# Down weights of the experts in 8 KB runs, with the expert block turned two columns apart

## What is computed

```
aff = softmax(h @ w_router);  gate, idx = top_k(aff.T, cap)      # cap = 2 * N / 16: 64 latent, 32 context
xe  = h[idx]                                                     # tokens of one expert
hid = silu(xe @ w_gate) * (xe @ w_up)                            # w_gate, w_up: 1024 x 1024
ye  = hid @ w_down * gate                                        # w_down: 1024 x 1024
y[idx] += ye
```

## Time and profile before

| what | value |
|---|---|
| median of 3 runs | 3875.69 us |
| lowest, highest | 3872.78, 3879.06 us |
| the profiled execution's own time | 3871.78 us |
| its span | 3869.7 us |
| DMA traffic of the weight stream's queue | 492.93 MB, 36.3% of 16 engines' span |
| expert loop of layer 0, layer 1 | about 1380 to 2310 us, 3283 to 3813 us |

### The profile page before, as it was taken

How to read it: one execution, slowest core, us unless ns; L and a number is a source line. 1 busy time by engine, 2 the same in 40 slices (tenths; PEclk the granted TensorE clock), 3 DMA queues, 4 the chain that set the end, 5 groups by cost and what they waited for, 6 DMA issues and landing times. The chain is left out here.

```text
span 3869.7 us, 40283 instructions
## 1 busy us (share of the span) xinstructions
PE 3226.1 (83%) x16642; PEld 2182.8 (56%) x16642; DVE 1115.7 (29%) x2003; ACT 550.4 (14%) x1054; POOL 449.7 (12%) x366
## 2 busy tenths in 40 slices
PE   7979996787879899999999984899946666899994
PEld 2545573787866386777776742665735563333331
DVE  0024422545424401111111114172047623111113
ACT  0133115222211100000000001041031200100010
POOL 0000000544403000000000003000026420000002
PEclk9979997899988689999999986999978785999998
DMA  9210112000014265566665650211100010999993
GB/s 303 92 39 17 34 45 86 1 1 1 1 49 131 76 217 192 200 223 212 214 229 190 214 192 24 63 33 33 55 22 1 11 44 15 383 382 362 388 378 142
DMA packets 200206, 512.50 MB, mean 132 GB/s; under 512 B 13200, under 2 KB 97424, under 8 KB 199696
## 3 DMA queue, kind: packets, MB, share of 16 engines
q1 hardware_dynamic: 192880, 492.93, 36.3%
q10 hardware_dynamic: 6048, 13.57, 1.0%
q0 software_dynamic: 1152, 4.19, 0.3%
HBM read 506.99 MB, written 3.67 MB: 132 GB/s over the span
## 5 line engine op out<-in xcount | busy, mean ns | idle before, releaser
L1961 PEld LDWEIGHTS bank<-arena,ring 128*128 128x128 f32 x4096 | 472.5, 195 | 34.5 <-issue 33.5
L1961 PE MATMUL bank<-arena,ring 128*128 128x96 f32 x4096 | 475.3, 278 | 0.8 <-DVE arena L2032 0.8
L1105 PE MATMUL bank<-arena 128*128 128x128 f32 x2208 | 271.9, 284 | 21.4 <-DVE arena L1277 19.7
L1105 PEld LDWEIGHTS bank<-arena 128*128 128x128 f32 x2208 | 264.3, 199 | 27.9 <-issue 24.6
L450 PE MATMUL bank<-arena,ring 128*128 128x384 f32 (+1 forms) x704 | 243.6, 509 | 8.9 <-DVEq L2287 7.5
L2100 PE MATMUL bank<-ring,arena 128*64 128x512 f32 x1024 | 233.4, 599 | 15.3 <-DMA ring<-in_moe_w_up_dram 8.3
L2040 DVE TENSOR_TENSOR arena<-arena,bank 128x512 f32<-128x512 f32 x160 | 110.0, 688 | 451.8 <-PE bank L1945 451.8
L1945 PE MATMUL bank<-arena 128*128 128x512 f32 (+1 forms) x320 | 187.3, 668 | 62.8 <-DVE arena L2040 60.1
L1991 PE MATMUL bank<-ring,arena 128*96 128x512 f32 x512 | 232.6, 606 | 2.2 <-DVE arena L2055 2.2
L1925 PE MATMUL bank<-arena,X 128*128 (+1 forms) x1024 | 165.9, 312 | 55.3 <-DVE arena L2032 26.6
L1925 PEld LDWEIGHTS bank<-arena,X 128*128 128x128 f32 x1024 | 143.7, 215 | 104.6 <-issue 35.0
(11 more groups left out here) (294 smaller groups left out, 3789.9 us busy)
## 6 DMA issues: line engine op xcount, KB each, us to landing
ring<-in_moe_w_gate_dram SPq DMA_DIRECT2D x128, 1024.0 KB, 5.1
ring<-in_moe_w_up_dram SPq DMA_DIRECT2D x128, 1024.0 KB, 5.3
ring<-in_moe_w_down_dram SPq DMA_DIRECT2D x128, 1024.0 KB, 7.0
ring<-in_w_mod_dram SPq DMA_DIRECT2D x48, 1024.0 KB, 5.3
ring<-in_odd_w_in_dram SPq DMA_DIRECT2D x16, 1024.0 KB, 5.6
ring<-in_even_w_in_dram SPq DMA_DIRECT2D x10, 1024.0 KB, 5.3
ring<-in_even_w_out_dram SPq DMA_DIRECT2D x4, 1024.0 KB, 5.4
arena<-in_rpb_tables_dram POOLq DMA_DIRECT2D x8, 512.0 KB, 4.5
```

The costliest lines, as they stand in the source:

```text
L1105: mm = nc.tensor.matmul(heads(out[:, :])[:, h, :], lhs(h), rhs(h), start=start, stop=stop)
L1961: mm = nc.tensor.matmul(bank[x + f // 4][:, (f % 4) * M:(f % 4 + 1) * M], wslot(c)[:, kk, f * P:(f + 1) * P], xe[:, k, :], start=k == 0 an ...
```

## The change

Down chunks are read so that partition p holds rows 2p and 2p + 1 of the chunk's 256, which lie next to each other in HBM: 8 KB in one run instead of two runs of 4 KB. For the down product the hidden features have to stand in the same order. `hidden_rows(f)` gives them: of each 256 hidden columns, the even ones for the first block and the odd ones for the second. In layer 0 the stationary blocks of gate and up (line 1961) are taken with it, in layer 1 the transposes' inputs (line 2116). Gate and up chunks are read as before. The products, their number and order, the waits and the slots are the same.

```diff
                 flat = t[w].rearrange("l e (k p) n -> (l e) p k n", p=P)
-                src = flat[bass.ds(l * NE + 2 * i + e, 1), :, 2 * c:2 * c + 2, :].rearrange("a p k n -> (a p) k n")
+                if w == "moe_w_down":
+                    rows = t[w].rearrange("l e (k p r) n -> (l e) p k r n", p=P, r=2)
+                    src = rows[bass.ds(l * NE + 2 * i + e, 1), :, c, :, :].rearrange("a p r n -> (a p) r n")
+                else:
+                    src = flat[bass.ds(l * NE + 2 * i + e, 1), :, 2 * c:2 * c + 2, :].rearrange("a p k n -> (a p) k n")
...
+            def hidden_rows(f):
+
+                return slice(f // 2 * 2 * P + f % 2, (f // 2 + 1) * 2 * P, 2)
...
                                     mm = nc.tensor.matmul(bank[x + f // 4][:, (f % 4) * M:(f % 4 + 1) * M],
-                                                          wslot(c)[:, kk, f * P:(f + 1) * P], xe[:, k, :],
+                                                          wslot(c)[:, kk, hidden_rows(f)], xe[:, k, :],
                                                           start=k == 0 and f % 4 == 0, stop=k == KB - 1 and f % 4 == 3)
...
-                            mm = nc.tensor.transpose(bank[5][:, b_ * P:(b_ + 1) * P], HID2[:, b_ * P:(b_ + 1) * P], ident)
+                            mm = nc.tensor.transpose(bank[5][:, b_ * P:(b_ + 1) * P], HID2[:, hidden_rows(b_)], ident)
```

## The result

The changed kernel takes 3903.14 us (median of 4, 3901.66 to 3909.53) against 3874.24 us for the kernel before (4 runs, 3871.91 to 3879.06): ratio 1.0076, 95% interval 1.0059 to 1.0094, so 23 to 36 us slower, where 3875.0 us and "no change" were forecast, with a range up to 3886. The execution shown here is the one of 3901.66 us, with a span of 3899.7 us.

A forecast was written before the change was run, and what follows sets the result against it. TensorE was taken to bound layer 0, and layer 1 nearly everywhere in a near tie with transfers. Median 3875.69 us + 0 (weight-load stride) + 0 (transposes) - 0.7 (down chunks) = 3875.0 us, range 3864 to 3886.

The forecast's parts named there:

- Part 1: Layer 0's up/gate weight loads, 4096 on TensorE's path: reading columns two apart was taken to cost 0.
- the ends of 0 and 457 us: Bounds for layer 0's 4096 strided loads: free, or twice the reading time at +0.1115 us each, +457 us.
- The partial end: Layer 0's strided weight loads costing 2% of a load-and-matmul pair, 4096 x 0.0022 = +9 us.
- Part 2: Layer 1's transposes, 64 strided loads of 141 ns: taken as free, +9 us if doubled.
- Part 3: Down chunks in runs of 8 KB, 64 a layer: 0.09 us saved a chunk, 0.7 us in all, layer 1 only.
- The pause in the steady pair: Layer 1, DMA engines nearly idle about 5 us a pair of experts; shorter down chunks would lengthen it about 0.4 us.
- The 0.7 us: Layer 1's saving: 8 down chunks ahead of waits, in the first pair and at the very end, 0.09 us each.
- the strided weight load is slower: Rival: layer 0's 4096 strided loads cost time on the path, up to 4341 us at full price; chance 0.14.
- The transfers gain far more: Rival: 8 KB packets or better HBM order remove layer 1's 15.2 us of weight waits, 3860.5 us; chance 0.07.
- arrive slower: Rival: down chunks take +0.20 us each, +13 us if all 64 are on the path, 3889 us; chance 0.03.
- nothing merges: Rival: down chunk runs stay 4 KB, so transfers don't change, 3875.7 us; chance 0.10.

The follow-up runs named there:

- e2: Changed kernel with down chunks back in runs of 4 KB, so both strides alone: 3896.97 us, ratio 1.0079 to the kernel before.
- e1: Changed kernel with both strides taken out, so down chunks in runs of 8 KB alone: 3866.26 us, ratio 0.9999 to the kernel before.
- e3: Kernel before with the stationary blocks of line 1961 taken with a step of four columns: 4491.00 us, ratio 1.1613.
- e11: Kernel before with the moving operand of line 1991 (512 columns) taken with a step of four columns: 4111.49 us, ratio 1.0628.

## Why the prediction was wrong

**Part 1, the stride in the weight loads, is the step that failed.** The place was right: 4096 loads on the path, multiplied without cover. Its price wasn't 0 but 6.2 ns a pair, 25 us, between the ends of 0 and 457 us; the interval of the whole loss, 23 to 36 us, holds it. I took the value from VectorE (2% within 9 ns, rows 6) as "the same memory read with the same 8-byte step". That row was read correctly and answers another question. For one operand, VectorE's call of 256 columns in 426 ns needs a line of two columns every 3.3 ns; TensorE wanted one every 1.74 (0.1115 / 64), and the limit found is 1.82. A slower reader that is not slowed says nothing of a faster one. That this is the reason is argued and not shown: both inputs of line 1548 have the step, and counted together they are a line every 1.66 ns. What VectorE's own limit is, no run here tells. The partial end, 2% of a pair, had no ground either: it copied VectorE's percentage. With that end the range stopped at 3886 and the rival that happened, with chance 0.14, lay outside it. For a term that is paid 4096 times, with bounds 457 us apart and one row of another engine between them, the range had to reach far past 0.2%.

The other 7 us of the profiled executions (936.3 - 904.2 = 32 in the loop) are the clock. Added up over the loop, 47 us ran at 1.2 GHz before and 68 after. From start to start within the line, 73 intervals lay in such stretches before and 162 after, at 0.216 us each in place of 0.118: 89 x 0.098 = 9 us. The 3867 at full clock give 3867 x 6 ns = 23 us. Together that is the 32. Whether the stride brought the lower clock stays open: in the runs that leave this line contiguous such intervals number 59 to 116, in e2, with the stride, 131.

The Trainium skill, "SBUF — State Buffer" (cachelines), gave both readings, and the trace decides between them with a number: two hits a line is almost enough, 0.92 ns a column (117.7 / 128) against 0.87 needed. The penalty for crossing lines is real for TensorE, and hidden only while it needs a line less often than every 1.82 ns.

**Part 2, the transposes:** the price was there, 65 ns a load, but nearly all of it under the matmuls. In e2 the 64 of them take 10.3 us in place of 9.7, so 0.6 us, where 0 was predicted and 9 was the bound.

**Part 3, the transfers:** right as far as can be told. Neighbouring rows merge (16384 packets fewer, as said), a down chunk is 4% shorter (0.11 us; 0.09 predicted), and e1 shows that it is worth nothing that can be measured. The pause in the steady pair took the saving as described: the DMA share of its 5 us fell from 0.29 to 0.21, 0.4 us, as predicted. The shorter chunk did nothing here, because the chunks between the pause and the waits of layer 1 are gate and up chunks. The 0.7 us in the first pair and at the end are too small to be told: the first pair of the changed kernel still has its eight waits of 0.61 to 0.63 us, and the last one went from 0.53 to 0.36 us.

**Rivals:** "the strided weight load is slower" is what happened, at 1/18 of its full price. "The transfers gain far more" and "arrive slower" are excluded by e1; "nothing merges" by the packet count.

## What to carry to other kernels

A column step in an operand of TensorE is not free because another engine reads it for free: for float32 count the 16-byte lines that the operand touches, times 1.8 ns, and compare with what one pass takes now. A stationary operand has the moving columns of the matmul as cover (512 hid even a step of four, 96 didn't hide a step of two); a moving one has none. And ask of a faster transfer which waits stand behind it before anything is given up for it.

## What the runs showed of the hardware

- Float32 columns reach TensorE at one 16-byte line per 1.81 to 1.87 ns on the weight side and per 1.76 ns on the moving side; contiguous columns (0.87 and 0.84 ns each) are not limited by it.
- This time for a line does not go with TensorE's granted clock: at step four a pair took 233 ns at 2.4 GHz and at 1.2 GHz (e3).
- At the lower clock level a step of two therefore costs nothing: in the kernel before and in e2, 5 us of the loop's first stretch at a granted 0.50 hold 24 matmuls each. Line 1961 before, line 1969 in e2 (columns as in e3's string):

```profile
1371.50:1376.50 5.00, 5.00 (x24) 5.00 (x25) 0.50 0.00 0
```

```profile
1361.30:1366.30 5.00, 5.00 (x24) 5.00 (x25) 0.50 0.00 0
```

- A slower operand read can take the clock with it: the granted clock of the loop was 0.97 contiguous, 0.96 at step two, 0.62 at step four (pairs of 0.234 us), yet 0.97 in e11, whose passes of 512 columns were twice as long as before. What decides between the two, these runs do not show.
